# An fp32 trunk of attention, pooling and experts: strided keys scored by residue class in quarters of the array, and another order at the end of attention

## The chip, the cores and the metric

The kernel runs on one core of a Trainium2 chip. The metric is the time of one execution in device microseconds; three executions of the kernel before took 1485.25, 1486.00 and 1486.94 us, a median of 1486.0.

## The reference, cut to what matters

256 tokens of width 1024 in fp32 pass through two layers. Layer 0 has dilated attention and a dense SwiGLU, layer 1 a pooling mixer and eight SwiGLU experts, of which each token uses two. Around them stand RMS norms and residual adds. The change touches the attention. For 16 heads of 64 it computes, in three groups g:

```python
WINDOWS = (128, 512, 2048); DILATIONS = (1, 4, 16)
qkv = (h @ w_qkv).reshape(B, S, N_GROUPS, 3, N_HEADS, HEAD_DIM)
for g in range(N_GROUPS):
    q = apply_rope(qkv[:, :, g, 0], cos, sin) * (HEAD_DIM ** -0.5)
    k = apply_rope(qkv[:, :, g, 1], cos, sin)
    o, lse = dilated_window_attention(q, k, qkv[:, :, g, 2], DILATIONS[g], WINDOWS[g] // DILATIONS[g])
wts = softmax(stack(lses, axis=0), axis=0)          # one softmax over the keys of all groups
out = sum(wts * outs) @ w_o
```

With 256 tokens the windows of groups 1 and 2 take in every earlier token at a distance that is a multiple of 4 or of 16. A query of group 1 therefore sees only the 64 keys of its own residue modulo 4, and one of group 2 sees keys that are among the same 64.

## The kernel before, in words

The tokens are permuted, so that the four residues modulo 4 lie in four blocks of 64; a row tile t of 128 tokens holds two of them. All products are made with numbers split into two fp32r halves (`w_hi`, `w_lo`, `a_hi`, `a_lo`), three matmuls for one (`product`, L386 to L390). Weights come from HBM in units of 1 MB: SP loads them (L402), ScalarE makes `w_hi` (L331), VectorE `w_lo` (L336). `RAW` = 4 raw units and `SPLIT` = 3 split ones are held; a `w_hi` waits until the unit three before has been used.

In the attention, 36 units of projections give rotated q and k (`qkT`, VectorE's L904 and L908, then GpSimd's add L496) and v (`v_sb`, ScalarE's L582). The work of a pair of heads (`side` 0 and 1) for one row tile is one step; there are N_STEP = 16. Attention itself is in plain fp32. A step has three parts:

- "scores" (PE L1360): for both sides, 256 keys of group 0, then the 128 keys of the own row tile for group 1 and for group 2, into a bank for each side. q and k lie on 64 partitions a side, so that the two sides stand in two row halves of the array. VectorE adds the mask and takes the maximum (L924), ScalarE the exponential (L594).
- "turn" (PE L1370): four transposes of 128x128 a side; ScalarE copies the result to `eT` (L602). VectorE inverts the sums and spreads them (`diag`, L942 and L944).
- "values" (PE L1380, L1385): one transpose of the spread inverses, and four products a side of 64 columns of `v_sb` with 128 columns of `eT`, the sides in two column halves of the array; VectorE multiplies (L938).

The order of all this is written out by hand in the list `ORDER`, which every engine walks through, each doing its share of an entry. Up to the last projection unit the parts of a step stand between units, about two units a step. Behind the last unit come steps 12 to 15 mixed with 16 "piece" entries: products of the attention's output with the output weights `U_WO` + 0 to 3, four pieces to a unit (`project`); VectorE adds each to x (L858). "turn out" splits the attention's output into `a_hi` (L570) and `a_lo` (L847). "turn x" transposes x (L1288) for the dense layer, after which ScalarE (L542) and VectorE (L836) split it. "split" makes `w_hi` and `w_lo` of a unit ahead of its use; `U_WO + 4` is the first dense unit `U_DENSE`.

The dense layer follows with `DENSE_SEQ`: first 0, second 0, first 1, second 1, down 0 and so on. A "first" unit uses the tiles 0 to 3 of turned x, for both row tiles t, a "second" unit the tiles 4 to 7. Behind the pooling mixer and the router come the experts: 8 times 42 units through a ring of 11 raw buffers.

Of the kernel before, what the change touches and what calls it, by code (L numbers as in the profile page):

```python
# [5 lines left out]
ALU = mybir.AluOpType  # L6
# [7 lines left out]
P = 128  # L14
# [13 lines left out]
E = 8  # L28
# [20 lines left out]
N_STEP = HEADS * TT // 2  # L49

# [57 lines left out]
for _u in range(N_QKV):  # L108
    ORDER.append(("unit", _u))
    _c, _i = divmod(_u, 3 * GROUPS)  # L110
    if _c:
# [3 lines left out]
        else:  # L115
# [6 lines left out]
          ("values", 12), ("piece", 4), ("split", U_WO + 3), ("turn", 13), ("scores", 14), ("piece", 5),  # L122
          ("values", 13), ("piece", 6), ("turn", 14), ("scores", 15), ("piece", 7), ("values", 14), ("piece", 8),
          ("turn", 15), ("piece", 9), ("values", 15), ("piece", 10), ("turn out", 3), ("piece", 11),
          ("piece", 12), ("piece", 13), ("split", U_WO + 4), ("piece", 14), ("turn x", 0), ("piece", 15),
          ("turn x", 1), ("split", U_WO + 5), ("split", U_WO + 6)]
# [10 lines left out]
def program(nc, x_in, xT_in, pool_scale, router, final_norm, units, expert_units, mask_in, cos_in, sin_in, ident_in, iota_in,  # L137
# [3 lines left out]
    with ctx:  # L141
# [25 lines left out]
        spare = sb("spare", [P, 8])  # L167
# [17 lines left out]
        s_sb = sb("s_sb", [P, 2, 4 * P], F32, attn)  # L185
        e_sb = sb("e_sb", [P, 2, 4 * P], F32, attn)
        eT = sb("eT", [P, 2, 4 * P], F32, attn)
        mask = sb("mask", [P, TT, 4 * P], F32, attn)
# [24 lines left out]
        fold = sb("fold", [P, E])  # L213
# [13 lines left out]
        slot_gate = sb("slot_gate", [P, 2])  # L227
        y_rows = rows[:, 1, :]
# [295 lines left out]
        def _(act):  # L524
# [49 lines left out]
            for kind, n in ORDER:  # L574
                if kind == "unit":
                    act.wait_ge(unit_used, n + 1)
                    if is_v(n):
# [19 lines left out]
                elif kind == "turn":  # L597
# [3 lines left out]
                    for side in range(2):  # L601
                        nc.scalar.activation(eT[:, side, :], ps[5 + side][:, :], ACT.Copy).then_inc(eT_ready, 1)  # L602
                elif kind == "turn out":
                    output_halves(n)
                elif kind == "split":
# [204 lines left out]
        def _(dve):  # L810
# [29 lines left out]
            def split_all(m, before_these):  # L840
                split_turned(m, before_these, range(KD))
# [47 lines left out]
            for kind, n in ORDER:  # L889
# [24 lines left out]
                elif kind == "scores":  # L914
# [4 lines left out]
                    for side in range(2):  # L919
# [4 lines left out]
                        nc.vector.tensor_tensor_reduce(out=s_sb[:, side, :], in0=ps[3 + side][:, :], in1=mask[:, t, :],  # L924
# [23 lines left out]
                elif kind == "piece":  # L948
                    add_piece(n)
                elif kind == "split":  # L950
# [850 lines left out]
```

## Time and profile before

| | |
|---|---|
| median of three runs | 1486.0 us |
| the profiled execution's own time | 1486.41 us |
| its span in the profile | 1484.6 us |
| PE, VectorE, ScalarE, GpSimd busy | 98%, 82%, 66%, 5% |
| mean granted TensorE clock | 0.996 |
| HBM traffic | 448.8 MB, 302 GB/s |

The span runs from the first to the last instruction; 1.8 us of the execution lie outside. PE stands for the matmuls, PEld for the loads of their stationary operand, DVE for VectorE, ACT for ScalarE, POOL for GpSimd, SP for the queue that issues transfers. A matmul's duration in the records is its time from start to end through the array, and such times overlap: what it costs when many follow is the distance between two starts. In a row of the timeline, equal instructions are merged; the second number is the time from the first one's start to the last one's end.

### The profile page before, as it was taken

Reading aid. Unit: us, or ns where it says so; the run is one execution under the profiler, and the core shown is the slowest. Engines: PE = TensorE matmul, PEld = TensorE weight load, DVE = VectorE, ACT = ScalarE, POOL = GpSimd, SP = SyncE. Lnnn points to the kernel's source line nnn. Section 1 sums busy time; section 2 is a strip of 40 time slices with the busy share of each in tenths; the row PEclk is TensorE's granted clock in tenths of the full one; section 3 lists DMA queues with packets and bytes.
Section 4 is the critical chain, followed back from the end, with each engine's and each line's share of the span. In section 5 each row is a group of like instructions: output and inputs, shape, how many; then the busy total and the mean of one; then the engine's idle time right before and its main releaser. Section 6 shows DMA issues by size and latency. Waiting matters only on the chain.

```text
span 1484.6 us, 20897 instructions
## 1 busy us (share of the span) xinstructions
PE 1453.4 (98%) x7790; PEld 1235.5 (83%) x7790; DVE 1218.9 (82%) x1068; ACT 974.5 (66%) x849; POOL 78.3 (5%) x65
## 2 busy tenths in 40 slices
PE   6999999999999899999999999999999999999996
PEld 6999999778888788888888888888888888888885
DVE  7788888774545689898899898898898989889886
ACT  5354444553444777777787777787777778778775
POOL 2311111100000000000000000000000000000000
PEclk9999999999999999999999999999999999999998
DMA  9544444355557499999999999999999999999980
GB/s 372 201 140 156 153 142 143 109 211 179 190 179 274 178 395 349 390 383 376 380 374 400 353 375 418 354 368 405 365 365 404 359 389 382 366 385 374 395 332 31
DMA packets 66714, 448.81 MB, mean 302 GB/s; under 512 B 7632, under 2 KB 9424, under 8 KB 14304
## 3 DMA queue, kind: packets, MB, share of 16 engines
q1 hardware_dynamic: 63120, 439.32, 76.5%
q0 software_dynamic: 3392, 8.69, 2.3%
q8 instruction: 38, 0.62, 0.2%
q14 instruction: 20, 0.16, 0.0%
q10 hardware_dynamic: 144, 0.02, 0.0%
HBM read 440.13 MB, written 7.86 MB: 302 GB/s over the span
## 4 chain that ended last, share of the span: by engine, by line
PE 95%; DVE 2%; ACT 1%; DMA 1%; issue 1%; SPq 0%; DVEq 0%; ACTq 0%
PE bank L388 30%; PE bank L390 29%; PE bank L389 29%; PE bank L1550 2%; PE bank L1385 1%; PE bank L1360 1%; PE bank L1370 1%; DMA raw<-in_units 1%; DVE w_lo L336 1%; PE bank L1559 0%; PE bank L1401 0%; PE bank L1527 0%; PE bank L1288 0%; DVE rot L908 0%; ACT rows L644 0%
## 5 line engine op out<-in xcount | busy, mean ns | idle before, releaser
L336 DVE TENSOR_TENSOR w_lo<-raw,w_hi 128x2048 fp32r<-128x2048 f32 x201 | 459.2, 2292 | 102.0 <-ACT w_hi L331 101.6
L331 ACT ACTIVATE w_hi<-raw 128x2048 fp32r<-128x2048 f32 x201 | 384.8, 1915 | 148.3 <-PE bank L390 140.1
L388 PE MATMUL bank<-w_hi,xg_hi 128*128 128x512 f32 x896 | 354.1, 395 | 1.7 <-DVE w_lo L336 1.0
L390 PE MATMUL bank<-w_hi,xg_lo 128*128 128x512 f32 x896 | 349.4, 390 | 0.0
L389 PE MATMUL bank<-w_lo,xg_hi 128*128 128x512 f32 x896 | 349.1, 390 | 0.0
L336 DVE TENSOR_TENSOR w_lo<-raw_late,w_hi 128x2048 fp32r<-128x2048 f32 x95 | 217.4, 2292 | 32.6 <-ACT w_hi L331 31.8
L336 DVE TENSOR_TENSOR w_lo<-raw_more,w_hi 128x2048 fp32r<-128x2048 f32 x95 | 217.2, 2291 | 21.7 <-ACT w_hi L331 21.2
L331 ACT ACTIVATE w_hi<-raw_more 128x2048 fp32r<-128x2048 f32 x96 | 184.9, 1926 | 49.8 <-PE bank L390 49.8
L331 ACT ACTIVATE w_hi<-raw_late 128x2048 fp32r<-128x2048 f32 x95 | 182.4, 1920 | 30.3 <-PE bank L390 30.3
L390 PEld LDWEIGHTS bank<-w_hi,xg_lo 128*128 128x128 f32 x896 | 168.2, 188 | 36.1
L388 PEld LDWEIGHTS bank<-w_hi,xg_hi 128*128 128x128 f32 x896 | 168.3, 188 | 35.8 <-issue 1.4
L389 PEld LDWEIGHTS bank<-w_lo,xg_hi 128*128 128x128 f32 x896 | 168.4, 188 | 33.7
L388 PE MATMUL bank<-w_hi,hT_hi 128*128 128x512 f32 x384 | 150.9, 393 | 0.0
L390 PE MATMUL bank<-w_hi,hT_lo 128*128 128x512 f32 x384 | 149.6, 390 | 0.0
L389 PE MATMUL bank<-w_lo,hT_hi 128*128 128x512 f32 x384 | 149.5, 389 | 0.0
L388 PE MATMUL bank<-w_hi,a_hi 128*128 128x256 f32 (+1 forms) x416 | 143.3, 345 | 0.3 <-DVE rot L908 0.3
L389 PE MATMUL bank<-w_lo,a_hi 128*128 128x256 f32 (+1 forms) x416 | 140.1, 337 | 0.0
L390 PE MATMUL bank<-w_hi,a_lo 128*128 128x256 f32 (+1 forms) x416 | 139.9, 336 | 0.0
L388 PE MATMUL bank<-a_hi,w_hi 128*128 128x256 f32 x384 | 111.5, 290 | 11.5 <-DVE w_lo L872 9.9
L389 PE MATMUL bank<-a_lo,w_hi 128*128 128x256 f32 x384 | 109.5, 285 | 0.0
L390 PE MATMUL bank<-a_hi,w_lo 128*128 128x256 f32 x384 | 109.4, 285 | 0.0
L388 PEld LDWEIGHTS bank<-w_hi,a_hi 128*128 128x128 f32 x416 | 78.8, 190 | 10.5 <-issue 1.2
(204 smaller groups left out, 1792.7 us busy)
## 6 DMA issues: line engine op xcount, KB each, us to landing
raw<-in_expert_units SPq DMA_DIRECT2D x128, 1024.0 KB, 7.0
raw_more<-in_expert_units SPq DMA_DIRECT2D x96, 1024.0 KB, 7.1
raw_late<-in_expert_units SPq DMA_DIRECT2D x96, 1024.0 KB, 7.0
raw<-in_units SPq DMA_DIRECT2D x73, 1024.0 KB, 4.8
hn<-in_expert_units SPq DMA_DIRECT2D x16, 1024.0 KB, 7.6
qkT<-in_xT SPq DMA_DIRECT2D x2, 512.0 KB, 4.5
raw<-in_units SPq DMA_DIRECT2D x2, 512.0 KB, 7.1
x<-in_x SPq DMA_DIRECT2D x1, 1024.0 KB, 9.7
```

The costliest lines, as they stand in the source:

```text
L331: nc.scalar.activation(w_hi[:, u % SPLIT, :], where, ACT.Copy).then_inc(hi_ready, 1)
L336: nc.vector.tensor_tensor(w_lo[:, u % SPLIT, :], home(u, i)[0], w_hi[:, u % SPLIT, :].bitcast(F32), ALU.subtract).then_inc(lo_ready, 1)
L388: nc.tensor.matmul(bank, hi, w[0], start=start, stop=False)
L389: nc.tensor.matmul(bank, hi, w[1], start=False, stop=False)
L390: return nc.tensor.matmul(bank, lo, w[0], start=False, stop=stop)
L1360: last = nc.tensor.matmul(ps[3 + side][:, at:at + kn], qkT[part, c % 2, 0, g, pair, t * P:(t + 1) * P], qkT[part, c % 2, 1, g, pair, k0:k0 ...
L1370: last = nc.tensor.transpose(ps[5 + side][:, k * P:(k + 1) * P], e_sb[:, side, k * P:(k + 1) * P], ident[:, :])
L1385: last = nc.tensor.matmul(ps[7][side * HD:(side + 1) * HD, 0:P], v_sb[:, c % 2, g, kt, col:col + HD], eT[:, side, k * P:(k + 1) * P], star ...
L1550: last = nc.tensor.transpose(ps[6][:, q * P:(q + 1) * P], h[:, q * P:(q + 1) * P], ident[:, :])
```

## The change

A query of group 1 or 2 is scored only against the 64 keys of its own block. The two blocks of a row tile are `half` 0 and 1; for each group, half and side there is one product of 64 queries with 64 keys over 64 partitions, which fills a quarter of the array. The 64 columns of group 1 and of group 2 lie side by side, and for half 1 in the other order. So a row of scores has 384 columns in place of 512 (`SEEN`). Turned, the last 128 columns hold on partitions 0 to 63 one group's keys and on 64 to 127 the other's, and `v_sb` is laid out to fit: `tile` 1 + half holds both groups' values for the keys of that half. The last two products of a side's values, 128 columns each, become two of 64 columns, each adding to its half of the output. Copies of v for groups 1 and 2 become two of 64 partitions where there was one.

The order at the end is another one: `w_lo` of `U_WO + 3` comes after step 14's scores, `w_hi` of `U_DENSE` ahead of piece 7 and its `w_lo` in two parts; "turn out 3" moves ahead of piece 10; the turning of x is in two halves on VectorE too, and PE makes the second half inside the first dense unit. `spare` grows by 32 bytes a partition, and `fold` is allocated further on.

```diff
+CLASS = P // 2
+SEEN = SEQ + 2 * CLASS
 ORDER += [("turn out", 0), ("scores", 12), ("piece", 0), ("piece", 1), ("turn out", 1), ("piece", 2),
           ("split", U_WO + 2), ("turn", 12), ("scores", 13), ("piece", 3), ("turn out", 2),
-          ("values", 12), ("piece", 4), ("split", U_WO + 3), ("turn", 13), ("scores", 14), ("piece", 5),
-          ("values", 13), ("piece", 6), ("turn", 14), ("scores", 15), ("piece", 7), ("values", 14), ("piece", 8),
-          ("turn", 15), ("piece", 9), ("values", 15), ("piece", 10), ("turn out", 3), ("piece", 11),
-          ("piece", 12), ("piece", 13), ("split", U_WO + 4), ("piece", 14), ("turn x", 0), ("piece", 15),
-          ("turn x", 1), ("split", U_WO + 5), ("split", U_WO + 6)]
+          ("values", 12), ("piece", 4), ("split hi", U_WO + 3), ("turn", 13), ("scores", 14), ("piece", 5),
+          ("split lo", U_WO + 3), ("values", 13), ("piece", 6), ("turn", 14), ("scores", 15), ("split hi", U_WO + 4),
+          ("piece", 7), ("values", 14), ("piece", 8), ("turn", 15), ("part lo", 0), ("piece", 9), ("values", 15),
+          ("turn out", 3), ("piece", 10), ("piece", 11), ("part lo", 1), ("piece", 12), ("piece", 13), ("piece", 14),
+          ("turn x", 0), ("piece", 15), ("split", U_WO + 5), ("turn x", 1), ("split", U_WO + 6)]
...
-        spare = sb("spare", [P, 8])
+        spare = sb("spare", [P, 16])
-        s_sb = sb("s_sb", [P, 2, 4 * P], F32, attn)
+        s_sb = sb("s_sb", [P, 2, SEEN], F32, attn)
...
-        fold = sb("fold", [P, E])
         xg_hi = sb("xg_hi", [P, KD, P], F32R)
...
         slot_gate = sb("slot_gate", [P, 2])
+        fold = sb("fold", [P, E])
...
                         for t in range(TT):
-                            last = nc.scalar.activation(v_sb[:, c % 2, g, t], ps[n % 2][:, t * QW:(t + 1) * QW],
-                                                        ACT.Copy, scale=rstd(0, t))
+                            for half in range(2):
+                                of = slice(half * CLASS, (half + 1) * CLASS)
+                                to = slice((half ^ (g == 2)) * CLASS, (half ^ (g == 2)) * CLASS + CLASS)
+                                if g == 0:
+                                    of, to, tile = slice(half * P, (half + 1) * P), slice(half * P, (half + 1) * P), 0
+                                else:
+                                    tile = 1 + half
+                                if g or half == 0:
+                                    last = nc.scalar.activation(v_sb[to, c % 2, tile, t], ps[n % 2][of, t * QW:(t + 1) * QW],
+                                                                ACT.Copy, scale=stat[of, 0, 6 + t:7 + t])
...
-            def split_all(m, before_these):
-                split_turned(m, before_these, range(KD))
+            def part_lo(half):
+
+                dve.wait_ge(hi_ready, U_DENSE + 1)
+                c = slice(half * UNIT // 2, (half + 1) * UNIT // 2)
+                part = nc.vector.tensor_tensor(w_lo[:, U_DENSE % SPLIT, c], home(U_DENSE)[0][:, c],
+                                               w_hi[:, U_DENSE % SPLIT, c].bitcast(F32), ALU.subtract)
+                if half:
+                    part.then_inc(lo_ready, 1)
...
-                elif kind == "turn x" and n:
-                    split_all(1, KD + QUARTERS)
+                elif kind == "turn x":
+                    split_turned(1, KD + QUARTERS, range(4 * n, 4 * n + 4))
...
-                    for g, at, k0, kn in ((0, 0, 0, SEQ), (1, SEQ, t * P, P), (2, SEQ + P, t * P, P)):
-                        for side in range(2):
-                            part = slice(side * HD, (side + 1) * HD)
-                            last = nc.tensor.matmul(ps[3 + side][:, at:at + kn],
-                                                    qkT[part, c % 2, 0, g, pair, t * P:(t + 1) * P],
-                                                    qkT[part, c % 2, 1, g, pair, k0:k0 + kn], start=True, stop=True)
+                    for side in range(2):
+                        part = slice(side * HD, (side + 1) * HD)
+                        nc.tensor.matmul(ps[3 + side][:, 0:SEQ], qkT[part, c % 2, 0, 0, pair, t * P:(t + 1) * P],
+                                         qkT[part, c % 2, 1, 0, pair, :], start=True, stop=True)
+                    for g in (1, 2):
+                        for half in range(2):
+                            own = slice(t * P + half * CLASS, t * P + (half + 1) * CLASS)
+                            at = SEQ + ((g - 1) ^ half) * CLASS
+                            for side in range(2):
+                                part = slice(side * HD, (side + 1) * HD)
+                                last = nc.tensor.matmul(ps[3 + side][half * CLASS:(half + 1) * CLASS, at:at + CLASS],
+                                                        qkT[part, c % 2, 0, g, pair, own], qkT[part, c % 2, 1, g, pair, own],
+                                                        start=True, stop=True)
...
-                        for k in range(4):
+                        for k in range(SEEN // P):
...
+                    near_keys(0)
+                    for half in range(2):
+                        own = slice(half * CLASS, (half + 1) * CLASS)
+                        for side in range(2):
+                            col = (2 * pair + side) * HD
+                            nc.tensor.matmul(ps[7][side * HD:(side + 1) * HD, own], v_sb[:, c % 2, 1 + half, t, col:col + HD],
+                                             eT[:, side, SEQ + half * CLASS:SEQ + (half + 1) * CLASS],
+                                             start=False, stop=False, skip_group_check=True)
+                    last = near_keys(1)
...
-                elif kind == "turn x":
-                    pe.wait_ge(wo_added, 4 * QUARTERS - 2 + 2 * n)
-                    turn(x, 2 * n)
-                    turn(x, 2 * n + 1)
+                elif kind == "turn x" and n == 0:
+                    pe.wait_ge(wo_added, 4 * QUARTERS - 2)
+                    turn(x, 0)
+                    turn(x, 1)
...
                     for t in range(TT):
+                        if s == 0 and t:
+                            pe.wait_ge(wo_added, 4 * QUARTERS)
+                            turn(x, 2)
+                            turn(x, 3)
```

`near_keys(k)` makes group 0's product with key tile k for both sides, 128 columns each. The mask is rebuilt on the host for the new columns.

## Rows read from the trace of the kernel before

**Rows 1.** The page: busy time of each engine, and the chain that ended last.
```profile
PE 1453.4 (98%) x7790; PEld 1235.5 (83%) x7790; DVE 1218.9 (82%) x1068; ACT 974.5 (66%) x849; POOL 78.3 (5%) x65
...
PE 95%; DVE 2%; ACT 1%; DMA 1%; issue 1%; SPq 0%; DVEq 0%; ACTq 0%
```
**Rows 2.** Windows: stretch, then length, busy time by engine, PEclk, DMA share, GB/s.
```profile
60.00:260.00 200.00, 200.00 (x1778) 193.93 (x1777) 166.61 (x242) 92.58 (x119) 29.10 (x20) 1.00 0.43 148
...
530.00:1484.00 954.00, 941.62 (x4286) 777.94 (x4284) 843.35 (x554) 716.76 (x528) 29.46 (x14) 1.00 0.93 364
```
**Rows 3.** Timeline of PE, 262 to 303 us, the two entries that waited.
```profile
278.25 0.30 PE L1380 MATMUL bank<-ident,diag 128*128 128x128 f32 x1 [1.05 <-DVE diag L944]
...
301.24 1.09 PE L1288 MATMUL bank<-ident,x 128*128 128x128 f32 x8 [0.78 <-DVE x L858]
```
**Rows 4.** Timeline of PE, 100 to 118 us: start, length, instruction.
```profile
100.99 0.27 PE L1380 MATMUL bank<-ident,diag 128*128 128x128 f32 x1
101.19 1.10 PE L1385 MATMUL bank<-eT,v_sb 128*64 128x128 f32 x16
102.22 1.15 PE L1360 MATMUL bank<-qkT 64*128 64x256 f32 x12
103.29 0.39 PE L388 MATMUL bank<-w_hi,a_hi 128*128 128x256 f32 x1
...
109.14 1.04 PE L1370 MATMUL bank<-ident,e_sb 128*128 128x128 f32 x8
```
**Rows 5.** Line L1385, 101 to 104 us: duration in ns, min/median/max.
```profile
L1385 PE MATMUL bank<-eT,v_sb x16: 272/273/324, 101.2 to 102.0; 128*64 128x128 f32 x16
```
**Rows 6.** The fold product in PE's timeline, and weight loads by shape (mean ns).
```profile
506.67 0.61 PE L1508 MATMUL bank<-fold,rows 128*128 128x8 f32 x4 [0.53 <-DVE rows L1074]
...
L1508 PE MATMUL bank<-fold,rows 128*128 128x8 f32 x4 | 0.6, 261 | 0.5 <-DVE rows L1074 0.5
...
L1508 PEld LDWEIGHTS bank<-fold,rows 128*128 128x128 f32 x4 | 0.5, 190 | 1.0 <-DVE rows L1074 1.0
...
L1385 PEld LDWEIGHTS bank<-eT,v_sb 128*64 128x64 f32 x256 | 13.7, 136 | 2.8 <-issue 2.2 <-ACT eT L602 0.3
```
**Rows 7.** The router's products: PE's timeline at 503.6 us, and their mean.
```profile
503.60 0.64 PE L1490 MATMUL bank<-hT,router_g 128*32 128x256 f32 x8
...
L1490 PE MATMUL bank<-hT,router_g 128*32 128x256 f32 x8 | 1.2, 391 | 0.1
```
**Rows 8.** Groups of VectorE (100 to 262 us) and ScalarE (0 to 262 us).
```profile
L924 DVE CUSTOM_DVE_ANT_0 s_sb<-bank,mask 128x512 f32<-128x512 f32 x20 | 13.8, 689 | 1.7 <-PE bank L1360 1.4 <-DVE hn L938 0.2
...
L582 ACT ACTIVATE v_sb<-bank,stat 128x256 f32<-128x256 f32 x24 | 10.1, 470 | 34.7 <-PE bank L390 34.7
```
**Rows 9.** VectorE's splits by their source, groups of the whole run.
```profile
L336 DVE TENSOR_TENSOR w_lo<-raw,w_hi 128x2048 fp32r<-128x2048 f32 x201 | 459.2, 2292 | 102.0 <-ACT w_hi L331 101.6
...
L336 DVE TENSOR_TENSOR w_lo<-raw_more,w_hi 128x2048 fp32r<-128x2048 f32 x95 | 217.2, 2291 | 21.7 <-ACT w_hi L331 21.2
```
**Rows 10.** Timeline of VectorE, 262 to 306 us.
```profile
275.47 2.29 DVE L336 TENSOR_TENSOR w_lo<-raw,w_hi 128x2048 fp32r<-128x2048 f32 x1
...
277.87 0.23 DVE L944 COPY diag<-softs 128x128 f32<-128x128 f32 x1
```
**Rows 11.** Timelines of ACT, DVE and PE around the first dense units.
```profile
298.66 1.57 ACT L542 ACTIVATE a_hi<-bank,gain_col 128x256 fp32r<-128x256 f32 x4 [4.96 <-PE bank L1288]
...
301.10 3.36 DVE L836 SCALAR_TENSOR_TENSOR a_lo<-bank,gain_col,a_hi 128x256 fp32r<-128x256 f32 x8
...
302.11 0.47 PE L388 MATMUL bank<-w_hi,a_hi 128*128 128x512 f32 x1
...
316.64 4.48 DVE L336 TENSOR_TENSOR w_lo<-raw,w_hi 128x2048 fp32r<-128x2048 f32 x2
...
318.74 0.60 PE L1401 MATMUL bank<-ident,dh 128*128 128x128 f32 x4
```
**Rows 12.** Window behind the router: columns as in rows 2.
```profile
509.50:513.00 3.50, 3.50 (x18) 3.50 (x18) 2.53 (x8) 1.90 (x5) 0.00 (x0) 0.51 0.99 407
```

More of the change, by code:

```diff
@@ L184, in program @@
         rot = sb("rot", [P, 2, 2 * SEQ], F32, attn)
-        s_sb = sb("s_sb", [P, 2, 4 * P], F32, attn)
-        e_sb = sb("e_sb", [P, 2, 4 * P], F32, attn)
-        eT = sb("eT", [P, 2, 4 * P], F32, attn)
-        mask = sb("mask", [P, TT, 4 * P], F32, attn)
+        s_sb = sb("s_sb", [P, 2, SEEN], F32, attn)
+        e_sb = sb("e_sb", [P, 2, SEEN], F32, attn)
+        eT = sb("eT", [P, 2, SEEN], F32, attn)
+        mask = sb("mask", [P, TT, SEEN], F32, attn)
         xT = qkT[:, 1].rearrange("p a g b t -> p (a g b t)")[:, 0:KD * SEQ]
@@ L601, in _ @@
                     for side in range(2):
-                        nc.scalar.activation(eT[:, side, :], ps[5 + side][:, :], ACT.Copy).then_inc(eT_ready, 1)
+                        nc.scalar.activation(eT[:, side, :], ps[5 + side][:, 0:SEEN], ACT.Copy).then_inc(eT_ready, 1)
                 elif kind == "turn out":
                     output_halves(n)
-                elif kind == "split":
+                elif kind in ("split", "split hi"):
                     split_hi(act, n)
@@ L923, in _ @@
                             dve.wait_ge(o_ready, n - 1)
-                        nc.vector.tensor_tensor_reduce(out=s_sb[:, side, :], in0=ps[3 + side][:, :], in1=mask[:, t, :],
+                        nc.vector.tensor_tensor_reduce(out=s_sb[:, side, :], in0=ps[3 + side][:, 0:SEEN], in1=mask[:, t, :],
                                                        scale=1.0, scalar=-3e38, op0=ALU.add, op1=ALU.max,
@@ L949, in _ @@
                     add_piece(n)
-                elif kind == "split":
+                elif kind in ("split", "split lo"):
                     split_lo(dve, n)
-                elif kind == "turn x" and n:
-                    split_all(1, KD + QUARTERS)
+                elif kind == "part lo":
+                    part_lo(n)
+                elif kind == "turn x":
+                    split_turned(1, KD + QUARTERS, range(4 * n, 4 * n + 4))
             dve.wait_ge(wo_added, 4 * QUARTERS)
@@ L1381, in _, with near_keys @@
                     pe.wait_ge(eT_ready, 2 * n + 2)
-                    for k, (g, kt) in enumerate(((0, 0), (0, 1), (1, t), (2, t))):
+                    def near_keys(k):
                         for side in range(2):
                             col = (2 * pair + side) * HD
-                            last = nc.tensor.matmul(ps[7][side * HD:(side + 1) * HD, 0:P],
-                                                    v_sb[:, c % 2, g, kt, col:col + HD],
-                                                    eT[:, side, k * P:(k + 1) * P], start=k == 0, stop=k == 3)
+                            last = nc.tensor.matmul(ps[7][side * HD:(side + 1) * HD, 0:P], v_sb[:, c % 2, 0, k, col:col + HD],
+                                                    eT[:, side, k * P:(k + 1) * P], start=k == 0, stop=k == 1)
+                        return last
+                    near_keys(0)
[7 more added lines that the diff above has]
+                    last = near_keys(1)
                     last.then_inc(pv_ready, 1)
@@ L1704, in shape_constants @@
     by16 = (dist >= 0) & (dist % 16 == 0)
-    mask = np.empty((TT, P, 4 * P), np.float32)
+    mask = np.empty((TT, P, SEEN), np.float32)
     for t in range(TT):
-        rows = slice(t * P, (t + 1) * P)
-        seen = np.concatenate([near[rows], by4[rows, rows], by16[rows, rows]], axis=1)
-        mask[t] = np.where(seen, 0.0, MASKED)
+        for half in range(2):
+            own = slice(t * P + half * CLASS, t * P + (half + 1) * CLASS)
+            strided = (by4[own, own], by16[own, own])
+            seen = np.concatenate([near[own], strided[half], strided[1 - half]], axis=1)
+            mask[t, half * CLASS:(half + 1) * CLASS] = np.where(seen, 0.0, MASKED)
     freq = (10000.0 ** (-np.arange(0, HD, 2, dtype=np.float32) / np.float32(HD))).astype(np.float32)
```

## The prediction

> **What bounds the kernel now.** I read the page's first parts first. TensorE is busy 1453.4 of 1484.6 us, VectorE 1218.9, ScalarE 974.5, and the chain that ended last lies 95% on PE [rows 1]. So what matters is how much TensorE time the change removes, and whether a new wait takes its place. The profiled execution took 1486.41 us (the span of 1484.6 and 1.8 around it), 0.4 above the median of 1486.0; I make the sum against it.
>
> Second, the stages. From 60 to 260 us (projections with attention steps between them) PE is busy 200.00 of 200 us, VectorE 166.61 and ScalarE 92.58, at a DMA share of 0.43. In the experts' 954 us PE is busy 941.62, at a DMA share of 0.93 [rows 2]. In the hand-ordered end of attention PE has two waits worth the name: 1.05 us on VectorE's diag (values of step 13) and 0.78 us on VectorE's x (the second half of turned x) [rows 3].
>
> Third, one attention step instruction by instruction; there are 16. An fp32 matmul leaves two records, a transpose one. The values run from 101.19 to 102.22: 1.03 us for 16 records, two side by side in the array, so eight pairs. The scores run from there to 103.29: 1.07 us for two pairs of 256 columns and four of 128. Eight transposes cover 1.04 us; one takes 0.27 (as L1380's), so they follow at (1.04 - 0.27) / 7 = 0.11 [rows 4].
>
> **A pair, and a change of tiling.** In the values the first record has 324 ns against 272 for the others: 0.05 us of weight load that nothing hides [rows 5]. From the transpose ahead of them (100.99) to the first (101.19) there are 0.20 us where 0.11 is the pitch [rows 4]. So a change of tiling costs 0.09 us and one exposed load, 0.14 with 64 weight columns. The values are then 0.14 + 8 x 0.11 = 1.02, near the 1.03 seen: a pair of 128 columns costs 0.11, and the scores' four such pairs 0.44.
>
> **What 64 columns cost.** No row has 64 moving columns. The nearest is the fold product, 8 moving columns over 128 weight columns: four records cover 0.61 us and one takes 0.26, so they follow at 0.12, no closer than those of 128 columns. There the weight load sets the pace. A load takes 190 ns for 128 weight columns and 136 for 64 [rows 6], 0.05 us less. Off a pitch of 0.11 that gives 0.06 us for a record with 64 weight and 64 moving columns. Bounds: 0.05 (half a pitch) and 0.11 (nothing saved). I take 0.06, since the load of that very shape is in the rows.
>
> **Part 1, transposes.** Six instead of eight: 2 x 0.11 = 0.22 us a step.
>
> **Part 2, values.** Four pairs of 128 columns stay, four become 64 columns: 4 x (0.11 - 0.06) = 0.20 (bounds 0 and 0.24). The tiling stays 128x64.
>
> **Part 3, scores.** The 256-column part stays. Four pairs (0.44) give way to 16 records in quadrants. The router's products have four column tiles in the array at once: eight records of 256 columns cover 0.64 us and each lasts 0.39, so the last starts 0.25 after the first, while one after another it would be seven times some 0.2 [rows 7]. If quadrants do the same, they make four rounds: 0.14 for the change of tiling (64x128 to 64x64) + 4 x 0.06 = 0.38, a gain of 0.06. Bounds: with no drain between these two, 4 x 0.05 = 0.20, a gain of 0.24; with two tiles at a time 0.14 + 8 x 0.06 = 0.62, a loss of 0.18.
> The rows show the drain where full-height and half-height tilings meet, and none between two modes that both have 64 rows. The Trainium skill (TensorEngine Tiling (Array Packing), Key Properties) says that changing the mode, not just the tile, drains the engine. By that rule 0.14 a step stays; if it doesn't hold here, the sum is 16 x 0.14 = 2.2 us lower. I keep the drain, since every change of shape that the rows do show has it.
>
> The step's sum is 0.22 + 0.20 + 0.06 = 0.48; x 16 = **7.7 us**. It reaches the end of the run, since PE waits for nothing in those 200 us, and VectorE at 83% has room for steps that come 3% faster.
>
> **Part 4, work on the other engines.** Mask, exponential and copy of eT go from 512 to 384 columns; the mask takes 689 ns [rows 8], a quarter off what grows with the columns is about 0.13 for each. Under projection units that is hidden. At the end of attention it shortens the chain from scores to transposes by about what PE's own work shrinks, so the cover stays. ScalarE's v copies go from 24 to 40; at up to 470 ns each [rows 8] that is 7.5 us over 260 in which it is half idle, and two units pass before anyone reads v: nothing. The mask's transfer is 128 KB shorter, in a queue that PE doesn't wait for then: nothing. The allocation moves tensors between `spare` and `fold` by 32 bytes. VectorE's split reads `raw`, which stays, at 2292 ns, and `raw_more`, which moves, at 2291 [rows 9]. Where a tensor lies changes nothing that I can see: zero, with a bound of 0.5 us either way.
>
> **Part 5, the order at the end.** (a) The w_lo of the last output unit, 2.29 us, stands behind diag of step 13 instead of ahead of it, so diag comes about 2 us before 277.87 [rows 10] and the 1.05 us wait goes. That unit is first read by piece 12, over 10 us on. Next late on VectorE are two masks (2 x 0.6), an add (0.7) and this w_lo (2.3); they are through before values 14.
> (b) The first dense unit's w_hi moves ahead, to a wait for piece 7 on ScalarE. Queued behind it is eT of step 15. Its 1.9 us lie under values 14, piece 8 and the transposes (about 3 us), so it costs nothing; without that cover it would cost 1.9. Its w_lo, in halves of 1.15 us, goes where VectorE waits for pieces.
> (c) The second half of turned x goes into the first dense unit. PE then starts this unit as soon as a first pair of a_lo exists: a_hi from 298.66 on at 0.39 each, a_lo at 0.42 each, so about 300.4 instead of 302.11 [rows 11]; the transposes that stood before it (0.87) come later, within it. Piece 15's add, now behind four a_lo, is done at 301.9, and PE asks for it at 303.1. So the 0.78 wait goes. Behind it stands a chain with little slack: w_hi, w_lo, squares, root, w_hi, table load, dsg, dh and the w_lo from 316.64 to 318.9, which PE reads at 319.1, behind the transposes of dh that start at 318.74 [rows 11]. PE comes 0.8 earlier; 0.3 of slack and 0.3 by which the chain moves up too (one w_hi is out of its way) cover 0.6. So (c) gives 0.6, and what is late next is this w_lo.
> Sum of the end: 1.05 + 0.6 = **1.7 us**.
>
> Total 7.7 + 1.7 = 9.4: 1486.4 - 9.4 = 1477.0 for an execution like the profiled one; the 0.4 to the median is less than I can tell, and I leave **1477.0 us**.
>
> **Rivals.**
> A, quadrants go two at a time, or 64 columns cost what 128 do. For it: no row has tiles halved both ways. Against: four column tiles overlap [rows 7], and so do row pairs and column pairs [rows 4]. Two at a time: 0.22 + 0.20 - 0.18 = 0.24, x 16 = 3.8, + 1.7: 1481. Rounds of four at 0.11: values 0, scores 0.44 - 0.14 - 0.44 = -0.14, so 0.08 x 16 + 1.7 = 3.0: 1483.4.
> B, slower: quadrant records follow one another. 16 x 0.06 + 0.14 = 1.10 against 0.44 is a loss of 0.66 a step, less 0.42: 0.24 x 16 - 1.7 = 2.1 more, 1488.5; at a pitch of 0.11 it is 1.90, 1.04 x 16 - 1.7 = 15 more, 1501. It decides from 0.44 + 0.42 + 0.11 = 0.97 us for a step's quadrants. The same overlaps speak against it.
> C, the gain is taken back later. If transfers paced the experts, PE would wait there for w_hi as much longer as it came earlier: 1486. For it: a DMA share of 0.93. Against: PE is busy 98.7% of that stage [rows 2].
> D, more than forecast: no drain in the scores and the eight 64-column rounds at 0.05, 0.22 x 16 = 3.5 us more. Besides, the granted clock is 0.51, the 1.2 GHz level, from 509.5 to 513.0 [rows 12], which costs about half of these 3.5 us; everything before it now comes 9 us earlier, and if this fall stays out, it is 1.7 less. 1472 to 1475.
>
> **How the numbers follow.** Forecast (1475 to 1480) 0.64; D 0.10; A 0.15; B 0.05; C 0.04; the rest 0.02. A measurement of this kernel tells 0.2% (3.0 us) from no change, so faster means below 1483.0: the forecast, D and most of A, 0.87. Within: C, the ends of A and B that are near it, 0.08. Slower 0.05. The range 1473 to 1482.5 leaves out the far ends of A and D, B and C.
>
> **What would show it.** Values of about 0.82 us up to the next work, scores of about 1.01, transposes at the same 0.11 but six of them; in the scores, 64-column records that start four at a time. Values 13 without a wait on diag; dense products between two groups of x transposes; at the fourth dense unit, near 309 us, a wait of up to 0.3 us on w_lo. PE's idle time in the experts unchanged. The forecast is wrong if quadrant records stand one behind the other, if a step's scores take over 1.2 us, or if PE gets idle time in the experts.

## The result, and the profile after

Four executions of the changed kernel took 1474.93 to 1475.77 us, a median of **1475.41 us**, against 1485.62 (four executions, 1484.63 to 1486.94) of the kernel before on the same chip: ratio 0.993, 95% interval 0.9917 to 0.9944. The change is 10.2 us faster; the forecast was 1477.0 with a range of 1473.0 to 1482.5. The profiled execution took 1475.32 us, its span is 1473.5.

The page, its busy times and the chain that ended last:
```profile
PE 1443.3 (98%) x7886; PEld 1224.8 (83%) x7886; DVE 1213.7 (82%) x1069; ACT 977.6 (66%) x865; POOL 78.3 (5%) x65
...
PE 95%; DVE 2%; ACT 1%; DMA 1%; issue 1%; SPq 0%; DVEq 0%
```
Beside [rows 1]: PE has 96 records more and is 10 us less busy, and the chain is as before 95% PE. So nearly all that was saved is TensorE work; its idle time fell by 1.0 us only, since a new wait took the place of two old ones.

One attention step in PE's timeline, as in [rows 4]:
```profile
99.94 0.27 PE L1405 MATMUL bank<-ident,diag 128*128 128x128 f32 x1
100.15 0.44 PE L1410 MATMUL bank<-eT,v_sb 128*64 128x128 f32 x4
100.42 0.40 PE L1419 MATMUL bank<-eT,v_sb 128*64 128x64 f32 x8
100.65 0.39 PE L1410 MATMUL bank<-eT,v_sb 128*64 128x128 f32 x4
100.97 0.70 PE L1377 MATMUL bank<-qkT 64*128 64x256 f32 x4
101.60 0.46 PE L1385 MATMUL bank<-qkT 64*64 64x64 f32 x16
101.99 0.39 PE L390 MATMUL bank<-w_hi,a_hi 128*128 128x256 f32 x1
...
107.85 0.82 PE L1395 MATMUL bank<-ident,e_sb 128*128 128x128 f32 x6
...
114.25 0.27 PE L1405 MATMUL bank<-ident,diag 128*128 128x128 f32 x1
```
The values run from 100.15 to 100.97, 0.82 us; the scores to 101.99, 1.02 us. The next step's L1405 comes at 114.25, 14.31 us after this one's; in the kernel before the same distance was 14.77. So a step became 0.46 us shorter. Duration of the quarter products, and of the 64-column values:
```profile
L1385 PE MATMUL bank<-qkT x16: 218/218/267, 101.6 to 101.8; 64*64 64x64 f32 x16
...
L1419 PE MATMUL bank<-eT,v_sb x8: 219/222/222, 100.4 to 100.6; 128*64 128x64 f32 x8
```
These are 16 records of eight products, as an fp32 product leaves two. All start within 0.25 us though each lasts 0.218: they stand in the array four at a time. The single records start 0.007 us apart within a round of four, and the rounds 0.058 us apart (the second 0.107 behind the first, whose load nothing hides).

Windows: the projections with their steps, the hand-ordered end up to the first dense unit, the experts (columns as in [rows 2]):
```profile
60.00:254.77 194.77, 194.77 (x1850) 185.91 (x1849) 163.78 (x242) 95.24 (x131) 29.27 (x20) 1.00 0.44 152
254.77:292.50 37.73, 36.15 (x295) 27.37 (x294) 29.64 (x68) 20.06 (x39) 3.76 (x5) 1.00 0.44 131
530.00:1472.00 942.00, 931.00 (x4243) 770.19 (x4241) 834.50 (x549) 709.02 (x523) 29.46 (x14) 1.00 0.93 364
```
PE never idles beside the projections. In the experts it is idle for 11.0 us, before 12.4 [rows 2]: nothing was taken back there. In the middle window it is idle for 1.58 us. PE's waits from 60 to 530 us, the largest (sum, times, longest):
```profile
PE bank L390 <- DVE a_lo L863: 1.4, 1, 1.4
PE bank L390 <- DVE w_lo L338: 1.4, 2, 1.0
```
Both waits of [rows 3] are gone. The wait on a_lo, 1.4 us, is new. The timelines of ACT, DVE and PE show how it arises:
```profile
255.09 1.92 ACT L592 ACTIVATE v_sb<-bank,stat 64x256 f32<-64x256 f32 x4 [3.64 <-PE bank L392]
257.04 0.63 ACT L572 ACTIVATE a_hi<-hn 128x512 fp32r<-128x512 f32 x1
...
257.70 0.69 DVE L863 TENSOR_TENSOR a_lo<-hn,a_hi 128x512 fp32r<-128x512 f32 x1 [1.22 <-ACT a_hi L572]
...
258.45 0.50 PE L390 MATMUL bank<-w_hi,a_hi 128*128 128x512 f32 x1 [1.44 <-DVE a_lo L863]
```
ScalarE finishes the last v unit's copies, now four of 64 partitions, and only then turns to a_hi, which PE's piece 0 needs by way of a_lo. The four take 1.92 us; in the kernel before, two copies of twice the height took 0.84.

Where the time came from, by how much earlier PE starts something than in the trace of before: what follows the last projection unit 5.67 us, piece 0 4.47, the first transposes of x 7.53, the second dense unit 8.20, the first product from dhT 7.71, the last one 9.28, the first product of the experts 9.32, their last from y 10.62; the whole span is 11.1 shorter. The step down at piece 0 is the new wait, and the one at the first dhT product is the wait on a w_lo of the dense layer. The steps up to 8.20 are the order at the end and the last four attention steps. The gains from 7.71 to 9.28 and from 9.32 to 10.62 are something that no part of the forecast has.

### The profile page after: what moved, and what is told of

Same layout as the page of the kernel before. It is cut to its first block, busy times and chain, and to the rows that moved or that the text cites. A ratio compares the mean times of both kernels' runs of the same rounds, so it can differ in the third digit from the quotient of the medians.

```text
span 1473.5 us, 21106 instructions
## 1 busy us (share of the span) xinstructions
PE 1443.3 (98%) x7886; PEld 1224.8 (83%) x7886; DVE 1213.7 (82%) x1069; ACT 977.6 (66%) x865; POOL 78.3 (5%) x65
## 4 chain that ended last, share of the span: by engine, by line
PE 95%; DVE 2%; ACT 1%; DMA 1%; issue 1%; SPq 0%; DVEq 0%
PE bank L390 30%; PE bank L392 29%; PE bank L391 29%; PE bank L1589 2%; DMA raw<-in_units 1%; PE bank L1395 1%; DVE w_lo L338 1%; PE bank L1377 1%; PE bank L1410 1%; PE bank L1598 0%; PE bank L1385 0%; ACT w_hi L333 0%; PE bank L1566 0%; PE bank L1436 0%; PE bank L1419 0%
```

## The experiments

Medians of the kernel before, taken with each experiment, were 1485.1 to 1485.6 us. Ratios are against it. A "start" of a tensor is its address within a partition.

**e1: the change without its allocation.**
```diff
-        spare = sb("spare", [P, 16])
+        spare = sb("spare", [P, 8])
...
+        fold = sb("fold", [P, E])
         xg_hi = sb("xg_hi", [P, KD, P], F32R)
...
         slot_gate = sb("slot_gate", [P, 2])
-        fold = sb("fold", [P, E])
```


> The changed kernel with spare and fold allocated as before, all else kept. Theory S (a stationary operand that starts 32 bytes off a multiple of 64 makes each 512-column product 0.0065 us longer, 0.2335 between starts instead of 0.2270): about 456 products have their stationary operand in dhT or in y_hi/y_lo, so 456 x 0.0065 = 3.0 us slower than the changed kernel, 1478.4, and down units of the dense layer take 5.60 us again instead of 5.44. Rival (as predicted, where a tensor lies changes nothing; the extra gain has another source): 1475.4, down units 5.44.

1477.77 us (5 executions, 1477.33 to 1478.74), ratio 0.9947 (0.9934 to 0.9961): 2.4 us slower than the change. The allocation, costed at zero, is worth more than the whole order at the end was forecast to be. Its place in the trace: both kernels start the first product from dhT at 316.97 us, and the last one at 475.59 here and at 474.03 in the change, 1.56 us apart over 240 products.

**e2: the allocation alone, in the kernel before.**
```diff
-        spare = sb("spare", [P, 8])
+        spare = sb("spare", [P, 16])
...
-        fold = sb("fold", [P, E])
         xg_hi = sb("xg_hi", [P, KD, P], F32R)
...
         slot_gate = sb("slot_gate", [P, 2])
+        fold = sb("fold", [P, E])
```


> The kernel before with the new allocation alone. Theory S: 3.0 us faster than before, 1482.6, with 0.227 us between the starts of products from dhT and y_hi; nothing changes ahead of the first down unit. Rival (the allocation changes nothing): 1485.6, starts 0.2335 apart.

1482.57 us (11 executions), ratio 0.998 (0.9971 to 0.9989): 3.0 us faster, as expected. The same products in the kernel before and in e2, from 345 to 460 us:
```profile
L390 PE MATMUL bank<-w_hi,dhT_lo 128*128 128x512 f32 x52 | 20.5, 394 | 0.0
```
```profile
L390 PE MATMUL bank<-w_hi,dhT_lo 128*128 128x512 f32 x52 | 20.2, 389 | 0.0
```
A product is 5 ns shorter in the mean; the starts are 0.2335 us apart before and 0.2270 here. The whole run has 240 such products with dhT and 216 with y: 456 x 0.0065 = 3.0 us.

**e3: only `spare` grows, `fold` stays.** By that, `xg_hi`, `xg_lo`, `hT_hi` and `hT_lo` move by 32 bytes too.
```diff
-        spare = sb("spare", [P, 8])
+        spare = sb("spare", [P, 16])
```


> The kernel before with spare grown to 16 and fold left where it is: now dhT and y_hi start on a multiple of 64 bytes, but everything behind fold (xg_hi, xg_lo, hT_hi, hT_lo) starts 32 bytes off. Theory S: 2688 products from xg and 1152 from hT at 0.0065 us more each, 25.0 us, less the 3.0 that dhT and y gain: 1485.6 + 22 = 1507.6. Rival (the place changes nothing): 1485.6. A third reading, that only the older tensors (dhT, y) are sensitive for another reason: 1482.6.

1503.89 us, ratio 1.0125 (1.011 to 1.0141): 18.3 us slower than before, from 32 bytes. Experts, 700 to 1300 us, of the kernel before and of e3:
```profile
L390 PE MATMUL bank<-w_hi,hT_lo 128*128 128x512 f32 x240 | 93.5, 390 | 0.0
```
```profile
L390 PE MATMUL bank<-w_hi,hT_lo 128*128 128x512 f32 x232 | 91.7, 395 | 0.0
```
And, as a control in the same trace, from 600 to 1400 us, the products from y, which stayed where e2 has it:
```profile
L389 PE MATMUL bank<-w_lo,y_hi x56: 389/389/389, 631.4 to 1365.6; 128*128 128x512 f32 x56
```
So the pace goes with the tensor and not with the run: starts 0.232 to 0.235 us apart for xg and hT, 0.227 for y and dhT. The mechanism is the expected one; the loss is 3.7 us less than the 22 expected, 3.1 of it because a product lost 0.0057 us in the mean and not 0.0065.

**e4: the class scoring alone, with the old allocation and the old order at the end.**
Against the change (all of its new order taken back, the allocation as in e1):
```diff
-          ("values", 12), ("piece", 4), ("split hi", U_WO + 3), ("turn", 13), ("scores", 14), ("piece", 5),
+          ("values", 12), ("piece", 4), ("split", U_WO + 3), ("turn", 13), ("scores", 14), ("piece", 5),
...
```


> The kernel before with the scoring by class alone: old allocation, old order at the end. Theory V (the second pair of v copies of the last v unit delays the first a_hi of the output by 1.08 us on ScalarE, and piece 0 waits for it): 16 steps at 0.47 are 7.5 us less, the new wait ahead of piece 0 adds 1.4, the old waits of 1.05 (diag) and 0.78 (x) stay: 1485.6 - 7.5 + 1.4 = 1479.5, and a wait of PE on a_lo of about 1.4 us ahead of piece 0. Rival (the wait ahead of piece 0 comes from the new order): 1478.1, no such wait.

1479.85 us, ratio 0.996 (0.9946 to 0.9974): 5.7 us faster than before. Its waits of PE from 230 to 345 us:
```profile
PE bank L390 <- DVE a_lo L863: 1.4, 1, 1.4
PE bank L1405 <- DVE diag L960: 1.2, 1, 1.2
PE bank L1306 <- DVE x L874: 0.8, 1, 0.8
```
So the new wait belongs to the class scoring, not to the order; diag and x are the two waits of [rows 3]. The order at the end is worth e4 less e1, 2.1 us by the medians; by the traces the first product from dhT comes 1.82 us earlier in e1 (316.97 against 318.79). The parts add up: 5.7 + 2.1 + 2.4 = 10.2.

**e5: the first half of a_hi ahead of the last v unit's copies.**
```diff
                 if kind == "unit":
                     act.wait_ge(unit_used, n + 1)
+                    if n == N_QKV - 1:
+                        output_halves(0)
...
-                elif kind == "turn out":
+                elif kind == "turn out" and n:
```


> The changed kernel, but on ScalarE the first a_hi of the attention's output stands ahead of the last v unit's four copies instead of behind them. Theory V (these copies are the new wait of 1.4 us ahead of piece 0): a_hi comes 1.9 us earlier, a_lo then waits for the values' two instructions on VectorE, PE's wait shrinks from 1.4 to about 0.2: 1475.4 - 1.2 = 1474.2. Rival (VectorE's queue sets the wait, the copies only stand beside it): wait unchanged, 1475.4. Second rival: the wait goes, but the v copies that end later, or a later wait on diag, take it back: 1475.4 with a wait elsewhere.

1473.83 us, ratio 0.9921 (0.9908 to 0.9935), 1.6 us less than the change. The largest wait of PE from 200 to 530 us is now
```profile
PE bank L390 <- DVE w_lo L338: 1.3, 2, 1.0
```
and none on a_lo is left. The wait cost what it shows, 1.4 us, within the spread of the executions.

**e6: group 0 in quarters as well**, so that a step's scores have one tiling (64x64) where they had two. The same numbers are computed.
```diff
-                    for side in range(2):
-                        part = slice(side * HD, (side + 1) * HD)
-                        nc.tensor.matmul(ps[3 + side][:, 0:SEQ], qkT[part, c % 2, 0, 0, pair, t * P:(t + 1) * P],
-                                         qkT[part, c % 2, 1, 0, pair, :], start=True, stop=True)
+                    for half in range(2):
+                        own = slice(t * P + half * CLASS, t * P + (half + 1) * CLASS)
+                        for side in range(2):
+                            part = slice(side * HD, (side + 1) * HD)
+                            nc.tensor.matmul(ps[3 + side][half * CLASS:(half + 1) * CLASS, 0:SEQ],
+                                             qkT[part, c % 2, 0, 0, pair, own],
+                                             qkT[part, c % 2, 1, 0, pair, :], start=True, stop=True)
```


> The changed kernel with the scores' 256 near keys in quarters of the array too (64 queries by 256 keys, four at a time, eight records of 256 columns instead of four), so that the scores need no change of tiling in their middle. Theory D (changing between 64x128 and 64x64 drains the array): the change costs 0.09 and an exposed load of 0.05, and the scores' first load is shorter by 0.05, 0.19 x 16 = 3.0 us less: 1472.4. Rival 1 (the drain comes with every new row of products, not with the tiling): 1475.4. Rival 2 (quarters of 256 columns don't go four at a time): two at a time adds 0.43 x 16 = 6.9: 1482.

1471.37 us, ratio 0.991 (0.9895 to 0.9925), 4.0 us less than the change. A step's scores in PE's timeline, up to the unit behind them:
```profile
100.22 0.66 PE L1379 MATMUL bank<-qkT 64*64 64x256 f32 x8
100.70 0.41 PE L1388 MATMUL bank<-qkT 64*64 64x64 f32 x16
101.04 0.38 PE L390 MATMUL bank<-w_hi,a_hi 128*128 128x256 f32 x1
```
From 100.22 to 101.04, 0.82 us where the change has 1.02 (100.97 to 101.99). 0.20 x 16 = 3.2 us; the drain between 64x128 and 64x64 was there, as forecast, and a single tiling avoids it. The single records of the two traces divide the 0.20: from the first record of group 0 to its second round 0.32 us in the change and 0.27 here, a shorter first load (0.05); from there to the quarters 0.31 and 0.21, the drain (0.10); from the quarters' first round to their second 0.107 and 0.056, the load that nothing hid (0.05). So the change of tiling itself costs 0.15 us. The Trainium skill (TensorEngine Tiling (Array Packing), Key Properties) says that changing the mode, not just the tile, drains the engine; this pair of runs agrees, with 0.15 us a step. The remaining 0.8 us were not traced. The kernel's own executions span 2.6 us, and three of its four had a mean granted clock of 0.997 or 0.998 where all four of the change had 0.996.

**e7: e5 and e6 together.**


> The two edits together: the first a_hi ahead of the v copies, and all scores in quarters. If both theories hold and the gains add: 1475.4 - 1.2 - 3.0 = 1471.2. If the waits at the end of attention take back what PE saves there (4 of the 16 steps), 1472.

1470.36 us, ratio 0.9898 (0.9883 to 0.9913): 5.05 us below the change, against 5.6 for the two gains one by one. The second expectation held in part: PE has two small waits at the end of attention that e5 has not, on diag and, ahead of piece 0, on a_lo.
```profile
PE bank L1410 <- DVE diag L962: 0.3, 1, 0.3
PE bank L390 <- DVE a_lo L865: 0.3, 1, 0.3
```

**e8: the quarters' order**, half, side, group in place of group, half, side, so that two neighbours use the same quarter.
```diff
-                    for g in (1, 2):
-                        for half in range(2):
+                    for half in range(2):
...
+                            for g in (1, 2):
```


> The changed kernel with the scores' strided products in another order: both groups of one quarter one behind the other, then the next quarter, so that neighbours share a quarter. Theory O (TensorE takes its matmuls in order; side by side go only neighbours in different quarters): five slots of a product's two passes at 0.058 instead of two, 0.58 instead of 0.23 us, 0.35 x 16 = 5.6 us more: 1481.0. Rival (the array sorts them itself): 1475.4.

1474.85 us, ratio 0.9929 (0.9914 to 0.9944): no loss that these executions show. PE's timeline:
```profile
100.90 0.70 PE L1377 MATMUL bank<-qkT 64*128 64x256 f32 x4
101.53 0.48 PE L1385 MATMUL bank<-qkT 64*64 64x64 f32 x16
101.94 0.39 PE L390 MATMUL bank<-w_hi,a_hi 128*128 128x256 f32 x1
```
The 16 records last from 101.53 for 0.48 us, 0.02 longer than in the change, 0.3 us over the 16 steps. The theory that an issue order of quarters is needed, with 0.35 a step, fell; neighbours in the same quarter cost nearly nothing.

**What is it about the 32 bytes?** The start of each tensor in its partition follows from the order and sizes of the allocations. In the change `w_hi`, `w_lo`, `a_hi`, `a_lo`, `dhT`, `y` start at 128 modulo 256 bytes and so do `xg` and `hT`; in the kernel before `dhT` and `y` start at 96, and in e3 `xg` and `hT` at 160. In the products of 512 columns the weights (`w_hi`, `w_lo`) are the moving operand and the other tensors named here the stationary one. That leaves open whether the stationary operand alone must stand well, or both, or the two relative to one another.

**e9: 32 bytes ahead of `w_hi` and 32 behind `w_lo`.**
```diff
+        sb("ahead", [P, 8])
         w_hi = sb("w_hi", [P, SPLIT, UNIT], F32R)
         w_lo = sb("w_lo", [P, SPLIT, UNIT], F32R)
+        sb("behind_w", [P, 8])
```


> The changed kernel with 32 bytes put ahead of w_hi and 32 behind w_lo, so that the split weights alone start 32 bytes off a multiple of 64. They are the moving operand of all products of the dense layer and the experts (512 columns) and of the v units, and the stationary one in 1152 products of 256 columns of the q and k units. Theory S (only the stationary operand's place counts): the q and k units get 1152 x 0.0065 = 7.5 us longer, 0.1265 between starts instead of 0.120, the experts stay at 0.227: 1475.4 + 7.5 = 1482.9. Rival M (any operand's place counts): about 5000 products of 512 columns more at 0.0065, 33 us on top: 1515. Rival L (a product of 256 columns hides it): 1475.4.

1498.41 us, ratio 1.0088 (1.0072 to 1.0105): none of the three expectations. By this edit w starts at 160 and all else at 192 (modulo 256), 32 apart. Experts from 700 to 1300 us, and projections from 100 to 230 us:
```profile
L394 PE MATMUL bank<-w_hi,hT_lo 128*128 128x512 f32 x237 | 93.7, 396 | 0.0
```
```profile
L394 PE MATMUL bank<-a_hi,w_lo 128*128 128x256 f32 x192 | 53.6, 279 | 0.0
```
The 512-column products are slow (396 against 390 ns), the 256-column ones of the projections *faster* than the change's 283. None of the three expected rules gives that. A rule on the two operands relative to one another does; so would one on where w stands that works opposite ways at 512 and at 256 columns, which the next run can tell apart.

**e10: 32 bytes ahead of `w_hi` only**, so that everything moves alike.
```diff
+        sb("ahead", [P, 8])
         w_hi = sb("w_hi", [P, SPLIT, UNIT], F32R)
```


> The changed kernel with 32 bytes ahead of w_hi and nothing taken back, so that every tensor behind raw starts 32 bytes off a multiple of 64, weights and activations alike. Theory R (what counts is whether the two operands of a product start alike modulo 64 bytes: alike 0.227 us for 512 columns and 0.120 for 256, unlike 0.2335 and 0.117): everything alike, 1475.4. Rival A (each operand off a multiple of 64 costs 0.0065 of its own at 512 columns): at least the 1498.4 of the weights alone. Rival P (one operand off is enough and the second costs nothing more): 1498 for 512 columns, starts 0.2335 apart.

1474.5 us, ratio 0.9925 (0.991 to 0.994), as the change:
```profile
L393 PE MATMUL bank<-w_hi,hT_lo 128*128 128x512 f32 x247 | 96.3, 390 | 0.0
```
Its projections are at 283 ns again, as the change's, though w starts at 160 as in e9. So it is not the absolute start, at the two places tried; both operands moved together keep the pace they had.

**e11: e7, with the projections' activations 32 bytes off** and, as was meant, all else where it stood.
```diff
-        a_hi = sb("a_hi", [P, KD * SEQ], F32R)
-        a_lo = sb("a_lo", [P, KD * SEQ], F32R)
+        a_hi_wide = sb("a_hi", [P, KD * SEQ + 16], F32R)
+        a_lo_wide = sb("a_lo", [P, KD * SEQ + 16], F32R)
+        a_hi, a_lo = a_hi_wide[:, 0:KD * SEQ], a_lo_wide[:, 0:KD * SEQ]
+        a_hi_off, a_lo_off = a_hi_wide[:, 8:8 + KD * SEQ], a_lo_wide[:, 8:8 + KD * SEQ]
...
```


> The kernel with all scores in quarters and the first a_hi ahead, and in it the activations of the 36 projection units at a place 32 bytes further on, inside a_hi and a_lo made 64 bytes wider, so that they start unlike the weights in the 1728 products of 256 columns and nowhere else. Theory R (unlike makes 256 columns 0.003 us shorter): 1470.4 - 1728 x 0.003 = 1465.2 at best, 0.117 between starts; by the sums of the weights-off run, 3.8 us less, 1466.6. Rival W (the gain at 256 columns hangs on the weights' place, not on the difference): 1470.4.

1492.64 us, ratio 1.0047 (1.0034 to 1.0061): missed. The last projection unit ended 3.7 us earlier than in e7 (some of it because e7's trace has a short fall of the clock near 20 us and this one has not), but 64 bytes more in each of two tensors moved `a_lo` by 64 and everything behind by 128, and the experts became slow:
```profile
L393 PE MATMUL bank<-w_lo,hT_hi 128*128 128x512 f32 x240 | 94.7, 395 | 0.0
```
A miss that says something. The tensors from `x` on stand 128 bytes unlike the weights, and their products are slow. `a_lo` stands 64 bytes unlike them, `a_hi` alike, and both serve the dense layer's products of 512 columns; from 345 to 460 us:
```profile
L394 PE MATMUL bank<-w_hi,a_lo x107: 389/397/398, 350.0 to 459.9; 128*128 128x512 f32 x107
```
The next start comes 0.236 us behind such a product with a_lo, and 0.228 to 0.229 behind one with a_hi. So operands 64 or 128 bytes apart are as slow as 32 apart. In the projections of this run a_hi stood 32 bytes and a_lo 96 bytes unlike the weights.

**e12: the same, 256 bytes wider in place of 64.**
```diff
-        a_hi_wide = sb("a_hi", [P, KD * SEQ + 16], F32R)
-        a_lo_wide = sb("a_lo", [P, KD * SEQ + 16], F32R)
+        a_hi_wide = sb("a_hi", [P, KD * SEQ + 64], F32R)
+        a_lo_wide = sb("a_lo", [P, KD * SEQ + 64], F32R)
```


> As e11, but a_hi and a_lo are made 256 bytes wider instead of 64, so that all tensors behind them keep their place modulo 256. The tensors' places in the program show that in e11 xg, hT, dhT and y started 128 bytes and a_lo 64 bytes unlike the weights modulo 256, while in the changed kernel all are alike modulo 256. Theory R256 (alike means modulo 256, not 64): the experts and the dense layer return to 0.227, the projections keep 0.117 to 0.118, and what e11 gained up to the last projection unit against e7, 3.6 us, stays: 1470.4 - 3.6 = 1466.8. Rival (the wider tensors slow the rest in another way): above 1490 again.

**1466.94 us**, ratio 0.9875 (0.9858 to 0.9891), 8.5 us below the change and the fastest of all. The last projection unit again ends 3.7 us earlier than in e7, and both traces have the short fall near 20 us. Experts and projections are both at their fast pace:
```profile
L393 PE MATMUL bank<-w_lo,hT_hi 128*128 128x512 f32 x240 | 93.4, 389 | 0.0
```
```profile
L394 PE MATMUL bank<-a_hi,w_lo 128*128 128x256 f32 x193 | 53.9, 279 | 0.0
```

## Why the prediction was right, point by point

The total was right within 1.6 us of a gain of 10.2. About half of the 1.6 is the base: the sum starts from the profiled execution's 1486.4, and the median of before is 1485.6. The step, which is most of the gain, was right in size and mechanism; two terms put at nothing were wrong, and a third was a little small.

- **The step.** Forecast 0.48, measured 0.46: values 0.82 (forecast 0.82), scores 1.02 (1.01), transposes 0.109 apart (0.11). Both guesses behind it held: 64 columns with 64 weight columns cost 0.058 (taken as 0.06), and quarters go four at a time. Sixteen steps give 7.4 us where 7.7 stood. Rivals A (two at a time) and B (one by one) fell by the starts of the quarter records, and B's switch point, 0.97 us for a step's quarters, is far from the 0.39 seen.
- **The drain.** 0.14 a step was kept, a price read off a change between two modes that are both 128 rows high; between 64x128 and 64x64 it is 0.15. e6 gets 0.20 back, 0.05 of it from the lighter first load of group 0. So this half of rival D fell in the change, and is there for the taking.
- **"V copies: nothing" failed.** The reason given was the engine's mean load and two units of distance to the reader of v. Both are true and beside the point: behind the last v unit's copies ScalarE has a_hi, the head of the hand-ordered end. Its copies last 1.92 us for the same data, since one of 64 partitions takes 472 ns and one of 128 takes 470 [rows 8]. Cost: 1.4 us, shown by e5.
- **"The allocation: zero, bound 0.5" failed, and by the most.** The check was on the wrong engine: VectorE's split took the same time at both places [rows 9], PE's products did not. Worth 2.4 us (change against e1) to 3.0 (e2). The rows of before held the sign of it: dhT's products took 394 ns beside 390 for those of hT with the same shape. The prediction did not ask why two groups of one shape differ.
- **The order at the end.** Forecast 1.7, measured 2.1 (e4 less e1). Both waits went; PE waits 0.4 us for the fourth dense unit's w_lo where up to 0.3 was forecast, at 311.38 instead of near 309:
```profile
311.38 0.50 PE L390 MATMUL bank<-w_hi,a_hi 128*128 128x512 f32 x1 [0.41 <-DVE w_lo L338]
```
  Of the surplus, 0.15 us is seen: with the class scoring, the old order's wait on diag is 1.2 us (e4), not 1.05. The rest is no larger than the spread of the executions, and by the traces' 1.82 us there is none.
- **Rival C** fell: PE's idle time in the experts went down, not up.

In sum: 7.4 (steps) - 1.4 (copies) + 2.1 (order) + 2.4 (allocation) = 10.5, against 10.2 measured. That the forecast's 9.4 came so close is in part luck: a cost of 1.4 us and a gain of 2.4 were both missed and nearly cancel.

## What to carry to other kernels

Cost a moved or split operation by what is queued behind it on its engine at the one place where the order is tight, not by the engine's mean load: on ScalarE a copy of 256 columns took 472 ns on 64 partitions and 473 on 128. Treat every edit of an allocation as an edit of all products whose operands it moves, list the mean of each product by name and shape before and after, and keep the two operands' starts alike modulo 256 bytes where 512 columns move; where 256 columns move, this kernel was faster with the starts unlike. When a stage is cut into smaller tiles, give the work beside it the same tiling, as one change of tiling (0.15 us here) costs more than two rounds of the smaller products (0.058 each).

## What the runs showed of the hardware that was not expected

**The pace of a product depends on where its two operands start relative to one another.** Starts alike modulo 256 bytes gave 0.227 us between products of 512 columns; 32, 64 or 128 apart gave 0.231 to 0.236 (e3, e9, e11). With 256 columns it is the other way round: 0.120 us alike, 0.116 to 0.119 at 32 or 96 apart (e9, e11, e12). Over this kernel's products that is 3 us (e2) to 18 us (e3). Three products in a row in PE's timeline, of e9 and of e12:
```profile
999.83 0.40 PE L392 MATMUL bank<-w_hi,xg_hi 128*128 128x512 f32 x1
...
1000.53 0.40 PE L392 MATMUL bank<-w_hi,xg_hi 128*128 128x512 f32 x1
```
```profile
1000.13 0.39 PE L392 MATMUL bank<-w_hi,hT_hi 128*128 128x512 f32 x1
...
1000.81 0.39 PE L392 MATMUL bank<-w_hi,hT_hi 128*128 128x512 f32 x1
```
0.70 us for three against 0.68. Why this is so was not found; distances other than these, and other numbers of columns, were not tried.

**Quarters overlap in both orders tried.** With two neighbours on one quarter (e8) the 16 records took 0.02 us longer.

**The short fall of the clock comes and goes.** It stands in the change's trace as in [rows 12], 9.3 us earlier, at the 1.2 GHz level:
```profile
500.20:503.70 3.50, 3.50 (x18) 3.50 (x18) 2.56 (x8) 1.90 (x5) 0.00 (x0) 0.52 0.99 405
```
Stretches from 15 to 27 us and from 495 to 520 us, of e5 and of e12 (the granted clock is the third number from the end):
```profile
15.00:27.00 12.00, 10.67 (x85) 10.30 (x85) 9.64 (x10) 5.74 (x3) 1.08 (x1) 1.00 1.02 406
495.00:520.00 25.00, 21.73 (x122) 17.91 (x119) 20.32 (x44) 18.88 (x27) 0.00 (x0) 1.00 0.81 325
```
```profile
15.00:27.00 12.00, 9.64 (x70) 9.45 (x70) 9.48 (x10) 5.74 (x3) 0.93 (x1) 0.86 1.03 411
495.00:520.00 25.00, 23.04 (x116) 19.08 (x115) 20.99 (x31) 18.44 (x20) 0.00 (x0) 1.00 0.93 380
```
In the profiles of the kernel before, of the change, e4, e8, e10 and e11 the clock falls to about half for some 3.5 us near the router (0.93 over that stretch); in those of e7, e9 and e12 near 20 us instead (0.86 there); in e1, e2, e3, e5 and e6 in neither place. The forecast put this in rival D, to be decided by whether work comes earlier; the change's profile has the fall though it comes 9 us earlier. In the 4.20 us ahead of it PE was busy for 2.93; in e5's trace a like stretch, 2.94 of 4.20 us from 494.00 on, is followed by no fall. Such a fall costs at most half of 3.5 us, about 1 to 2 us that no edit explains, so places behind it can be compared only between profiles that both have it, as those of before and of the change do, or both lack it. What decides whether it comes stays open.
